# Column sums of the modulation, taken one by one between the weight products

## The reference

```python
mod = silu(c) @ ada_w[layer] + ada_b[layer]       # 6 * 1024 numbers
shift1, scale1, gate1, shift2, scale2, gate2 = split(mod, 6)
x = x + gate1 * mixer(rmsnorm(x) * (1 + scale1) + shift1)
x = x + gate2 * ffn(rmsnorm(x) * (1 + scale2) + shift2)
```

## Time and profile before

| | |
|---|---|
| Median of 3 runs | 1481.65 us (1479.13 to 1483.35) |
| Profiled execution | 1484.93 us, of which span 1483.1 us |
| PE busy | 1427.2 us, 96% of the span |
| DVE busy | 1129.8 us, 76% |
| ACT busy | 773.7 us, 52% |
| TensorE clock, mean share granted | 0.986 |

### The profile page before, as it was taken

One profiled execution on the slowest core, in us unless ns is written; L12 is line 12 of the kernel. 1 busy time (PEld: TensorE's weight loads), 2 busy tenths in 40 slices (PEclk: granted clock), 3 DMA queues, 4 the chain that ended last, 5 costly groups with the idle time before them and its releaser, 6 DMA issues.

```text
span 1483.1 us, 21046 instructions
## 1 busy us (share of the span) xinstructions
PE 1427.2 (96%) x8355; PEld 1227.5 (83%) x8355; DVE 1129.8 (76%) x1244; ACT 773.7 (52%) x829; POOL 4.1 (0%) x7
## 2 busy tenths in 40 slices
PE   3999899999999999999999999999999999999999
PEld 2976799799798788888888888787887787899997
DVE  5798678776779876889898988988786777555544
ACT  1535333333555564777767777776664443443332
POOL 0000000000000000000000000000000000000000
PEclk9999899999999998999999999999999999999999
DMA  8868368876684472999998999974543335345642
GB/s 299 293 242 288 123 207 275 301 276 223 232 266 168 152 266 79 329 339 315 354 342 305 363 336 342 336 277 138 209 173 129 117 129 170 119 158 193 198 163 106
DMA packets 198431, 345.82 MB, mean 233 GB/s; under 512 B 11633, under 2 KB 90065, under 8 KB 193233
## 3 DMA queue, kind: packets, MB, share of 16 engines
q1 hardware_dynamic: 190320, 338.71, 66.3%
q10 hardware_dynamic: 8032, 6.01, 1.3%
HBM read 343.65 MB, written 1.05 MB: 232 GB/s over the span
## 4 chain that ended last, share of the span: by engine, by line
PE 52%; DVE 5%; issue 2%; ACT 2%; DVEq 0%; ACTq 0%
PE ps L1312 16%; PE ps L1313 15%; PE ps L1314 15%; DVE wlo L2103 2%; ACT whi L634 1%; PE ps L1958 1%; PE ps L1998 1%; DVE HL L2955 0%; PE ps L1371 0%; PE ps L1981 0%; DVE acc L2945 0%; PE ps L1517 0%; PE ps L1518 0%; PE ps L1431 0%; PE ps L1509 0%
## 5 line engine op out<-in xcount | busy, mean ns | idle before, releaser
L634 ACT ACTIVATE whi<-raw 128x2048 fp32r<-128x2048 f32 (+2 forms) x220 | 404.0, 1837 | 380.4 <-PE ps L1314 232.8
L2103 DVE TENSOR_TENSOR wlo<-raw,whi 128x2048 fp32r<-128x2048 f32 (+2 forms) x220 | 480.2, 2193 | 153.5 <-ACT whi L634 147.5
L1312 PE MATMUL ps<-whi,AH 128*128 128x512 f32 (+1 forms) x816 | 322.7, 395 | 3.6 <-DVE wlo L2103 2.2
L1313 PE MATMUL ps<-wlo,AH 128*128 128x512 f32 (+1 forms) x816 | 313.8, 385 | 0.0
L1314 PE MATMUL ps<-whi,AL 128*128 128x512 f32 (+1 forms) x816 | 313.7, 384 | 0.0
L1312 PE MATMUL ps<-AH,whi 128*128 128x256 f32 x896 | 256.2, 286 | 5.4 <-DVEq L2209 2.9
L1313 PE MATMUL ps<-AL,whi 128*128 128x256 f32 x896 | 255.0, 285 | 0.0
L1314 PE MATMUL ps<-AH,wlo 128*128 128x256 f32 x896 | 254.9, 284 | 0.0
L1312 PEld LDWEIGHTS ps<-whi,AH 128*128 128x128 f32 x816 | 154.9, 190 | 41.7 <-DVE wlo L2103 10.9
L1312 PEld LDWEIGHTS ps<-AH,whi 128*128 128x128 f32 x896 | 173.3, 193 | 7.7 <-DVEq L2209 3.6
L1314 PEld LDWEIGHTS ps<-whi,AL 128*128 128x128 f32 x816 | 154.7, 190 | 28.6
(11 more groups left out here) (345 smaller groups left out, 1432.2 us busy)
## 6 DMA issues: line engine op xcount, KB each, us to landing
raw<-in_ada_w SPq DMA_DIRECT2D x48, 1024.0 KB, 5.6
raw<-in_w_in SPq DMA_DIRECT2D x26, 1024.0 KB, 5.0
raw<-in_moe_w_up SPq DMA_DIRECT2D x24, 1024.0 KB, 7.1
raw<-in_h_w_in SPq DMA_DIRECT2D x16, 1024.0 KB, 5.5
raw<-in_moe_w_gate SPq DMA_DIRECT2D x16, 1024.0 KB, 7.1
raw<-in_moe_w_down SPq DMA_DIRECT2D x16, 1024.0 KB, 5.6
acc<-in_moe_w_down SPq DMA_DIRECT2D x16, 1024.0 KB, 7.3
raw<-in_m_w_in SPq DMA_DIRECT2D x12, 1024.0 KB, 5.8
```

Source lines behind the costliest of these rows:

```text
L634: act.activation(whi[:, h, 0:n], raw_at[s][:, 0:n], ACT.Copy).then_inc(w_hi, 1)
L1312: pe.matmul(o, sh, mh, start=first, stop=False)
L1313: pe.matmul(o, sh, ml, start=False, stop=False)
L2103: dve.tensor_tensor(wlo[:, h, 0:n], raw_at[s][:, 0:n], whi[:, h, 0:n].bitcast(fp), ALU.subtract)\
```

## The change

`three` and `m_unit` get a hook `beside`, called after each product. A class `ColumnSums` holds the list of sums of a burst and issues one of them at each call. Place 1: the 16 sums stand behind the first 16 products of `m_unit(first_bank, 4)`. Place 2: the 16 sums stand behind the first 16 of the 18 products of the first group's last unit. Place 3: the gate rows come first; the 8 sums stand behind the first 8 products of the next unit, and DVE reads gate rows first, then columns. The number of sums and their operands are the same.

```diff
-          (17, 1): ((1, "c"), (1, "g"))}
+          (17, 1): ((1, "g"), (1, "c"))}
...
-            def three(o, sh, sl, mh, ml, first, last):
+            def three(o, sh, sl, mh, ml, first, last, beside=lambda: None):
                 pe.matmul(o, sh, mh, start=first, stop=False)
+                beside()
                 pe.matmul(o, sh, ml, start=False, stop=False)
-                return pe.matmul(o, sl, mh, start=False, stop=last)
+                beside()
+                ins = pe.matmul(o, sl, mh, start=False, stop=last)
+                beside()
+                return ins
...
+            class ColumnSums:
+                def __init__(self, bank, at, n, done):
+                    self.bank, self.at, self.n, self.done, self.f = bank, at, n, done, 0
+                def one(self):
+                    if self.f == self.n:
+                        return
+                    sums, c0 = self.at(self.f)
+                    ins = pe.matmul(ps[:, self.bank, self.f:self.f + 1], sums[:, c0:c0 + 128], ones[:, 0:1],
+                                    start=True, stop=True)
+                    self.f += 1
+                    if self.f == self.n:
+                        ins.then_inc(self.done, 1)
...
-            def group(w, between=lambda: None):
+            def group(w, between=lambda: None, at_end=lambda: (lambda: None)):
...
-                        m_unit(w, bank, k0, nk, FT, HH, HL, by_tile=c == 1 and k0 == KS[-1][0])
+                        last = c == 1 and k0 == KS[-1][0]
+                        m_unit(w, bank, k0, nk, FT, HH, HL, by_tile=last, beside=at_end() if last else lambda: None)
...
             normed_half(1)
             pe.wait_ge(ada_used, 20)
-            ada_cols(sum_bank, 0, acc[:, 1, :], 1024, 8)
-            ada_cols(sum_bank, 8, acc[:, 2, :], 0, 8).then_inc(ada_sum, 1)
-            m_unit(w, first_bank, 4, 4, KT)
+            sums = ColumnSums(sum_bank, lambda f: (acc[:, 1, :], 1024 + 128 * f) if f < 8 else (acc[:, 2, :], 128 * f - 1024),
+                              16, ada_sum)
+            m_unit(w, first_bank, 4, 4, KT, beside=sums.one)
             m_unit(w, second_bank, 4, 4, KT, by_tile=True)
...
-            group(w, second_gate)
-            pe.wait_ge(ada_used, 32)
-            ada_cols(pair(w), 0, acc[:, 0, :], 0, 16).then_inc(ada_sum, 1)
+            def next_shift():
+                pe.wait_ge(ada_used, 32)
+                return ColumnSums(pair(w), lambda f: (acc[:, 0, :], 128 * f), 16, ada_sum).one
+
+            group(w, second_gate, next_shift)
             group(w)
...
-                sums, n0 = ((acc[:, 1, :], 1024), (late_sums, 0))[c]
-                ada_cols(h_step_bank(n), 0, sums, n0, 8).then_inc(l_mm, 1)
+                if c == 0:
+                    ada_cols(h_step_bank(n), 0, acc[:, 1, :], 1024, 8).then_inc(l_mm, 1)
+                    return
+                late.append(ColumnSums(h_step_bank(n), lambda f: (late_sums, 128 * f), 8, l_mm))
...
-                    m_unit(w, out_banks[c], k0, 4, KT, HH, HL, by_tile=c == 1 and k0 == 4)
+                    m_unit(w, out_banks[c], k0, 4, KT, HH, HL, by_tile=c == 1 and k0 == 4,
+                           beside=late[0].one if late else lambda: None)
...
-            columns_out(1)
             gates_out(1)
+            columns_out(1)
```

More of the change, by code:

```diff
@@ L1339, in m_unit @@
             def m_unit(w, bank, k0, nk, kts, sh=AH, sl=AL, s0=0, n=512, tiles=TT, t0=0, between=lambda: None,
-                       by_tile=False):
+                       by_tile=False, beside=lambda: None):
                 u, h = w.next_unit()
@@ L1351, in m_unit @@
                         ins = three(ps[:, bank + i, 0:n], sh[:, s0 + kk, cut], sl[:, s0 + kk, cut], wh[:, k, :], wl[:, k, :],
-                                    kk == 0, kk == kts - 1)
+                                    kk == 0, kk == kts - 1, beside)
                     if i == 0:
@@ L1802, in column_sums @@
                 pe.wait_ge(ada_used, 40 + 8 * c)
-                sums, n0 = ((acc[:, 1, :], 1024), (late_sums, 0))[c]
-                ada_cols(h_step_bank(n), 0, sums, n0, 8).then_inc(l_mm, 1)
+                if c == 0:
+                    ada_cols(h_step_bank(n), 0, acc[:, 1, :], 1024, 8).then_inc(l_mm, 1)
+                    return
+                late.append(ColumnSums(h_step_bank(n), lambda f: (late_sums, 128 * f), 8, l_mm))
+            late = []
             def h_steps(u, end):
@@ L2721, in _ @@
             h_lo(19)
+            gates_out(1)
             columns_out(1)
-            gates_out(1)
             first_out = w.unit - 4
```

## The result

Five runs of the changed kernel took 1486.62 to 1495.08 us, median 1490.87, against 1481.65 before (1479.13 to 1483.35). The ratio is 1.0057, with a 95% interval of 1.0036 to 1.0077: slower. The forecast was 1484.0, +0.16%, with a range of 1479.5 to 1488.5; the first median lies outside it, and a loss of over 0.3% had a chance of 0.29. The medians of the second measurement were 1487.82 against 1482.6.

The account below looks back on a forecast made before the run. PE, busy 96% of the span, was taken as the bound. Place 1 +3.3, place 2 -1.6, place 3 0 gave +1.7 us; 0.7 for timed runs with fewer clock drops made it +2.4, 1484.0 us, range 1479.5 to 1488.5.

Parts of the forecast that it names:

- Place 1, the step that failed: Place 1: uncovered wait, then a 3.4 us clock drop, remaining pairs at full clock; loss 3.3 us.
- Rival 1: Place 1: the clock does not come back while sums and products alternate; +8.1 there, 1488 in all; chance 0.15.
- The covered wait: Place 1: the burst had covered DVE's writing of `AL`; with sums inside the unit, PE idles 2.9 us.
- Rival 5: Place 1: no wait, `AL` done in time; both clock drops gone, 1478.5; chance 0.05.
- rival 2: Place 1: no clock drop in spite of the wait; +1.7 there, 1482 in all; chance 0.12.
- DVE's queue behind the sums: Place 1: DVE's columns, `lo` and portion delay the residual; its last tile starts 3.3 us later, DVE 0.4 behind PE.
- Sums, 0.22 us each in the new place: All 40 sums: two 0.11 us weight loads lie bare per sum, as in the burst; no gain, no loss.
- rivals 3: All places: weight loads hidden under products, sums at 0; -7.1 us, 1474.6; chance 0.09.
- 4 (0.33): All places: sums dearer, 0.33 us each, by a third bare load; +6.2 in all, 1488; chance 0.12.
- Place 2, -1.6, and place 3, 0: Place 2: clock drop behind the burst avoided, gain 1.6 us. Place 3: same price for sums, nothing late, 0.
- A delay before that stretch moves all of it.: From 200 to 240 us loads set the pace, started by DVE's progress, so an earlier delay is not absorbed.
- The sum: Place 1 +3.3, place 2 -1.6, place 3 0: +1.7 us; with 0.7 for missing drops, +2.4.

Follow-up runs that it names:

- a2: Changed kernel with only place 1 changed, places 2 and 3 keeping the bursts of the kernel before; ratio 1.0045.
- b3: Kernel before at places 1 and 3; at place 2 an extra burst of 16 unused sums ahead of the alternating sums and products; ratio 1.0075.
- b1: Only place 1 changed, with 6 filler matmuls keeping PE busy in the wait for `AL`; ratio 1.0013.
- b2: Changed kernel, but at place 1 transposes go first and the sums alternate in the first half's second_bank unit, with no wait before them; ratio 0.9979.
- b4: Only place 1 changed: sums alternate with products of the unit before the transposes, and the wait for `AL` follows; ratio 1.0022.
- c1: Repeat of the rearranged kernel: all three places changed, place 1's transposes ahead of the unit holding the sums; ratio 0.9978.
- c2: Only place 1 changed, transposes ahead of the unit holding the sums; bursts at places 2 and 3 as before; ratio 0.9979.
- c3: Only place 1 changed: wait for `AL`, a plain unit, then the sums among the products of the unit behind it; ratio 1.0062.
- a1: The changed kernel measured again without edit (the second measurement); median 1487.82 against 1482.6, ratio 1.0030.
- a3: Changed kernel with place 1's burst restored, only places 2 and 3 changed; ratio 0.9989.
- a4: Kernel before with the wait for `AL` moved ahead of place 1's burst, nothing alternating; ratio 1.0037.

## Why the prediction was wrong

**Place 1, the step that failed.** The prediction put it as: "3.41 us at 0.86, 4.0 pairs; the remaining 10.2 at 0.45". The wait (2.67 us, 2.9 counted), the drop that follows it, the price of a pair at either clock (0.453 and 0.85, counted as 0.45 and 0.86) all came as written. What did not come was the return of the clock after those 3.41 us, with 10.2 pairs still to run. Once down, it stayed down until the sums were over: 13.5 us in the changed kernel, 16.9 in a2, and 20.2 in b3, where a burst had lowered it and no wait was there. Where PE came to it busy and at full clock, the same alternation kept it (place 1 in b1, b2, b4, c1, c2 and c3; places 2 and 3 in the changed kernel, a1, a3, b2 and c1). In the changed kernel too the first pairs ran at full clock, but behind the wait, and it fell after 1.2 us. The loss was 7.7 us, counted as 3.3. Rival 1 had this course and +8.1 for it, with a chance of 0.15. The argument used against it, that half of PE's time is real streaming, was an opinion: no row of before showed such a mixture at the lower clock. What in the alternation keeps the clock down, its weight loads or the little that it streams, is not separated by any run.

**The covered wait.** This was right and is the root: the burst had lain over the writing of `AL`. Uncovered, the wait costs +2.9 us with plain products behind it (b4) and +6.2 with the whole burst behind it (a4). Rival 5 is out. So is rival 2: the clock did fall.

**DVE's queue behind the sums.** Counted as the later one by 0.4 us; in fact PE was the later one by 1.04. Five of its eight plain products behind the sums ran at the lower clock too, 1.0 us more than was counted.

**Sums, 0.22 us each in the new place.** Right: 0.226. With it rivals 3 (loads covered) and 4 (0.33) are out. The generous reading of the Trainium skill (TensorE: Matmul & The Clock Gate, "LDWEIGHTS — get the stationary operand into the array") is not borne out for loads in a row: the one right behind a product was covered, the two after it lay bare.

**Place 2, -1.6, and place 3, 0.** Right against this execution: -1.4 and 0.0. As an average the gain is a little larger, since the burst of place 2 drew a different drop each time. Seven profiles have it: in one there was no drop (a4), in three one of 3.4 us behind the burst (before, b1, c3), in three one of 6.8 us that began within the burst (a2, b4, c2). From the last unit to the second of the next group they took 13.4, 14.9 and 16.5 us. The alternation took 13.45 in all five profiles that have it there, never with a drop, so the mean gain is 1.9 us. At place 3 the prediction's own terms end at 551.2 and not at 551.4; in the trace DVE still idled for 1.40 us before `out_matrix`, where it had idled for 2.07, so nothing was late.

**"A delay before that stretch moves all of it."** That none of it is absorbed was right, but not for the reason given. Loads did not set the pace from 200 to 240: PE was busy for 40.00 of the 40.00 us in the earlier trace rows. Of the 7.7 us, 6.3 were left when the first group's unit 16 began, and the 1.5 between are the clock drop at 245.5, which of these two executions only that of the kernel before had; PE's waits for `wlo` were 3.1 us in both. Over the eleven other profiles this stretch differs from before by -1.9 to +1.4 us, with and without a delay ahead of it.

**The sum.** By the parts of the two profiles, 7.7 - 1.4 is +6.3 us. By the means of all profiles it is much the same: 8.3 at place 1 (7.7, 7.7 and 9.4) less 1.9 at place 2, +6.4. The timed difference was +9.2 in the first measurement and +5.2 in the second. What made the first one longer by 4 stays open: neither profiled execution of the changed kernel (1486.62 and 1486.72) was that slow. The drops differ from one execution to the next at place 1, at place 2 and elsewhere, so a sum over single executions is good for 2 us at best.

## What to carry to other kernels

Before moving small instructions off an engine's path, look at what wait they lie over: a burst that takes 3.5 us but covers a 2.9 us wait costs 0.6, besides a drop behind it. Here the sums among the products were harmless where PE came from dense products and expensive right after a wait; that order alone turned +0.3 to +0.6% into -0.2%. When PE is "busy" without a gap and yet late, look at the granted clock. One weight load hides behind a product, not three, so interleaving single-column matmuls saved none of their own time, only the clock drop behind the burst.

## What the hardware showed that was not expected

- The lower clock lasted at least as long as sums and products alternated: 13.5, 16.9 and 20.2 us at 0.85 us a pair, though PE was busy without a gap. The same pairs (0.453 us) behind dense products never lowered it, over 7 us at a time, in nine profiles. With plain 512-column products the clock returned after 3.4 us (b4, c3).
- A burst of 32 load-bound instructions took 3.5 us at full clock and 6.3 us when the clock fell about 0.7 us into it (a4). In the alternation a sum costs 0.226 us at full clock and 0.42 at the lower one (0.85 less 0.43 for the product): weight loads slow down with the clock as products do.
- The same burst of place 2 drew no drop in one execution, one of 3.4 us in three and one of twice that in three.
- With PE idle for 2.6 to 2.7 us behind the transposes the clock fell in all six profiles that have this wait (after, a1, a2, a4, b4, c3).
